# Two hybrid blocks on one core: the mixers' projections and gates as three products of rounded parts, in another order

## What is computed

```python
h = z @ w_in
(q_a, k_a, v_a, r_a, lr_f, lr_b, q_b, k_b, v_b, g_a, g_b) = jnp.split(h, SPLIT_POINTS, axis=-1)
a = gla_branch(q_a, k_a, v_a, r_a, lr_f, lr_b, gla_w2, gla_b2, gla_gn)
b = attention_branch(q_b, k_b, v_b, q_norm, k_norm, cos, sin)
y = (jax.nn.sigmoid(g_a + b_merge[0]) * (a @ w_pa)
     + jax.nn.sigmoid(g_b + b_merge[1]) * (b @ w_pb))
return y @ w_out
```

## Time and profile before

| | us |
|---|---|
| runs of the kernel | 2798.41, 2788.34, 2796.54 |
| median | 2796.54 |
| the profiled execution | 2796.98 |
| its span, first to last instruction | 2795.2 |
| TensorE busy | 2577.6 (92%) |
| VectorE busy | 1010.1 (36%) |
| ScalarE busy | 824.5 (29%) |
| GpSimd busy | 902.2 (32%) |
| mean granted TensorE clock | 0.965 |

### The profile page before, as it was taken

How to read it: one execution, slowest core, us unless ns; L and a number is a source line. 1 busy time by engine, 2 the same in 40 slices (tenths; PEclk the granted TensorE clock), 3 DMA queues, 4 the chain that set the end, 5 groups by cost and what they waited for, 6 DMA issues and landing times.

```text
span 2795.2 us, 46739 instructions
## 1 busy us (share of the span) xinstructions
PE 2577.6 (92%) x18898; PEld 2057.0 (74%) x18898; DVE 1010.1 (36%) x2406; ACT 824.5 (29%) x1416; POOL 902.2 (32%) x373
## 2 busy tenths in 40 slices
PE   7999999999999999999989799998978679999997
PEld 7997567999999766799989555555558575555554
DVE  3411433543442153354245532323234533232233
ACT  4431212444433131254433221221123522212112
POOL 6870002788788100178867000000016230000000
PEclk9999989999999999999999899999988989999999
DMA  7545321554654522145554899999963058999996
GB/s 236 170 157 148 118 58 61 162 170 158 189 181 146 152 98 61 61 151 183 173 143 125 330 417 421 421 421 422 421 206 103 19 215 353 421 421 421 422 421 258
DMA packets 287879, 644.01 MB, mean 230 GB/s; under 512 B 35584, under 2 KB 209792, under 8 KB 238336
## 3 DMA queue, kind: packets, MB, share of 16 engines
q1 hardware_dynamic: 284672, 635.79, 61.5%
q10 hardware_dynamic: 2176, 3.15, 0.4%
q0 software_dynamic: 896, 3.15, 0.4%
HBM read 637.85 MB, written 4.19 MB: 230 GB/s over the span
## 4 chain that ended last, share of the span: by engine, by line
PE 80%; DMA 10%; DVE 6%; ACT 2%; issue 1%; SPq 0%; ACTq 0%; POOL 0%; DVEq 0%
PE bank L558 37%; DMA wring<-in_exp_w 10%; PE bank L522 10%; PE bank L1088 6%; PE bank L1066 6%; PE bank L652 5%; PE bank L1099 3%; PE bank L1045 3%; PE bank L1058 3%; PE bank L740 1%; PE bank L591 1%; PE bank L813 1%; DVE ARENA L1919 1%; DVE XN_rounded L1527 1%; PE bank L532 1%
## 5 line engine op out<-in xcount | busy, mean ns | idle before, releaser
L1976 POOL TENSOR_TENSOR wring_rounded<-wring,wring_rounded 128x1024 fp32r<-128x1024 f32 (+1 forms) x336 | 873.7, 2613 | 320.2 <-ACT wring_rounded L1159 319.7
L558 PE MATMUL bank<-SQ_rounded,wring_rounded 128*128 128x272 f32 (+1 forms) x3456 | 647.9, 288 | 28.9 <-POOL wring_rounded L1976 18.0
L558 PEld LDWEIGHTS bank<-SQ_rounded,wring_rounded 128*128 128x128 f32 x3456 | 544.5, 190 | 31.2 <-POOL wring_rounded L1976 14.0
L558 PE MATMUL bank<-XN_rounded,wring_rounded 128*128 128x272 f32 (+1 forms) x1728 | 496.2, 287 | 0.0
L1159 ACT ACTIVATE wring_rounded<-wring 128x1024 fp32r<-128x1024 f32 (+1 forms) x336 | 374.7, 1116 | 351.7 <-PE bank L558 343.3
L558 PE MATMUL bank<-ARENA_rounded,wring_rounded 128*128 128x272 f32 (+1 forms) x3456 | 438.3, 289 | 9.5 <-DVE ARENA_rounded L1735 4.2
L558 PEld LDWEIGHTS bank<-ARENA_rounded,wring_rounded 128*128 128x128 f32 x3456 | 433.6, 190 | 12.7 <-DVE ARENA_rounded L1735 4.4
L558 PEld LDWEIGHTS bank<-XN_rounded,wring_rounded 128*128 128x128 f32 x1728 | 329.1, 190 | 0.1
L1088 PE MATMUL bank<-wring,ARENA 128*32 128x512 f32 x2048 | 246.2, 598 | 41.0 <-DVE ARENA L1919 30.2
L1427 ACT ACTIVATE ARENA<-bank 128x512 f32<-128x512 f32 x128 | 76.4, 597 | 672.3 <-PE bank L1088 672.3
L1066 PE MATMUL bank<-ARENA 64*128 64x256 f32 x2048 | 255.7, 389 | 1.6 <-ACT ARENA L1419 1.6
(11 more groups left out here) (242 smaller groups left out, 2455.9 us busy)
## 6 DMA issues: line engine op xcount, KB each, us to landing
wring<-in_exp_w SPq DMA_DIRECT2D x256, 1024.0 KB, 18.3
ARENA<-in_exp_w SPq DMA_DIRECT2D x128, 1024.0 KB, 16.8
wring<-in_ffn_w_gate SPq DMA_DIRECT2D x44, 1024.0 KB, 5.5
wring<-in_ffn_w_up SPq DMA_DIRECT2D x44, 1024.0 KB, 8.1
wring<-in_ffn_w_down SPq DMA_DIRECT2D x32, 1408.0 KB, 6.2
wring<-in_w_in SPq DMA_DIRECT2D x14, 2048.0 KB, 7.8
wring<-in_conv_w_in SPq DMA_DIRECT2D x24, 512.0 KB, 5.4
wring<-in_attn_w_in SPq DMA_DIRECT2D x5, 2048.0 KB, 8.0
```

Of the source, the lines that this page charges most:

```text
L558: ins = nc.tensor.matmul(o, rounded(a_[:, k, cols]), rounded(x), start=(start and k == 0 and j == 0), stop=(stop and k == len(tiles) - 1 a ...
L1976: st.done(nc.gpsimd.tensor_tensor(rounded(low), low, part(high), ALU.subtract), wl_ready)
```

## The change

The products of in4, in0, in1, in2 and of the gates become three products of rounded parts. Their chunks (16 for the projections, 16 for the gates in each layer) enter the plan of chunks; ScalarE makes the high parts, VectorE the low parts (a new `low_part`), with their own semaphore. The mixer's input is split too: ScalarE rounds XN into SQ, VectorE subtracts SQ from XN in place once the float32 products of in3 are done. v_a is now computed by channel in four tiles, copied out, and turned by TensorE into the layout by token. The key product of in3 goes first, the decays' products ahead of the queries; the means come after the first GLA tile, the swaps after v_a. Squares, QB, XR, OSTD and KET get other places in memory. On ScalarE absolute value, exponential and logarithm are put between the GLA tiles, and the three high parts of pb go to the steps 22, 24 and 26. VectorE's chain of norms, decays and rotations is reordered with low parts between them. GpSimd makes two pb low parts ahead of the last attention output's, and one after it.

```diff
+ROUNDED_BY_VECTOR = ("in4", "in0", "in1", "in2", "gate")
+QUERY_BANKS, KEY_BANK, GLA_BANKS = (2, 0, 4, 5), 1, (3, 6, 7, 3)
+VALUE_BANKS, TURN_BANKS, R_BANKS = (6, 7, 3, 6), (7, 3, 6), (7, 3, 6, 7)
+NORM_ORDER = ((4, KEY_BANK),) + tuple(enumerate(QUERY_BANKS))
...
+GATE_HIGHS = [1] + [n + 1 for n in range(STEPS) for g in GATES_DONE[n] if 2 <= g <= 12]
...
+                    low, high = chunk_views(c)
+                    pe.wait_ge(*low_at[c])
                     for k in range(KD):
-                        ins = nc.tensor.matmul(bank[b][:, 0:T], v[:, k, m * P:(m + 1) * P], XN[:, k, :], start=(k == 0),
-                                               stop=(k == KD - 1))
+                        for j, (a_, x) in enumerate(((low, SQ), (high, XN), (high, SQ))):
+                            ins = nc.tensor.matmul(bank[b][:, 0:T], rounded(a_[:, k, :]), rounded(x[:, k, :]),
+                                                   start=(k == 0 and j == 0), stop=(k == KD - 1 and j == 2))
...
+                tiles = pairs(SQ, XN, KD)
+                for m, b in enumerate(QUERY_BANKS):
+                    split_products(b, "act", tiles, "dve", (lambda k: st.need(xn_ready)) if m == 0 else None)
+                for m, b in enumerate(GLA_BANKS):
+                    split_products(b, "act", tiles)
+                    if m == 0:
+                        for i, mb in NORM_ORDER:
+                            products(mb, "act", None, [[(bank[mb][:, 0:T], const("mean64"), S2[:, i, :])]])
+                for b in VALUE_BANKS:
+                    split_products(b, "act", tiles)
+                for i, b in NORM_ORDER:
                     st.need(d2p)
-                products(i, "dve", "dve", [[(bank[i][:, 0:T], const("swap"), XR[:, i, :])]])
+                    products(b, "dve", "dve", [[(bank[b][:, 0:T], const("swap"), XR[:, i, :])]])
+                st.need(a2p)
+                for b, (a_, nt) in zip(TURN_BANKS, TILES):
+                    turns(b, "act", "act",
+                          [(bank[b][0:nt, m * P:(m + 1) * P], VT[:, m, a_:a_ + nt]) for m in range(4)])
+                for b in R_BANKS:
+                    split_products(b, "act", tiles)
...
+                for m, b in enumerate(R_BANKS):
                     st.need(bank_full["act"][b])
                     st.done(A(RA[:, m, :], bank[b][:, 0:T], ACT.Silu), bank_free["act"][b])
+                    high_part()
                 st.need(d2a)
                 A(QD[:, 0], BC[:, 0:2, :], ACT.Exp)
...
-                    if n in (22, 23, 24):
+                    if n in (22, 24, 26):
                         high_part()
...
+            def low_part():
+                c = next(vector_chunks)
+                low, high = chunk_views(c)
+                dve.wait_ge(wh_ready, c + 1)
+                st.done(TT(rounded(low), low, part(high), ALU.subtract), wv_ready)
...
+                low_part()
                 st.need(a2d)
                 for d in range(2):
                     st.done(STT(QD[:, d], QD[:, d], 0.125, QK[:, 0:2, :], ALU.mult, ALU.mult))
                     st.done(TT(KI[:, d], KI[:, d], QK[:, 2:4, :], ALU.mult))
                     st.done(TT(KE[:, d], KE[:, d], QK[:, 2:4, :], ALU.mult), gla_ready if d else None)
+                    low_part()
+                low_part()
+                low_part()
```

More of the change, by code:

```diff
@@ L268, in chunk_plan @@
         kind = label[0]
-        if kind == "up":
+        if kind in ROUNDED_BY_VECTOR:
+            for m in range(4):
+                add(label, lambda buf, m=m: buf[:, :].rearrange(
+                    "p (k n) -> p k n", k=KD)[:, :, m * P:(m + 1) * P], KD, P)
+        elif kind == "up":
             for ft in range(2):
@@ L431, in build_model @@
         chunks = chunk_plan(plan)
+        by_vector = [c[0][0] in ROUNDED_BY_VECTOR for c in chunks]
+        low_at = []
+        for c in range(len(chunks)):
+            n_vector = sum(by_vector[:c + 1])
+            low_at.append((wv_ready, n_vector) if by_vector[c] else (wl_ready, c + 1 - n_vector))
         def chunk_views(c):
@@ L673, in mixer @@
                 used(("in3", l))
-                v = cols_of(("in4", l), 512)
-                for m in range(4):
-                    products(4 + m, "act", "dve",
-                             [[(bank[4 + m][:, 0:T], v[:, k, m * P:(m + 1) * P], x) for k, x in enumerate(rows(XN))]])
-                used(("in4", l))
-                v = cols_of(("in0", l), 512)
-                for m in range(4):
-                    products(m, "act", "act",
-                             [[(bank[m][:, 0:T], v[:, k, m * P:(m + 1) * P], x) for k, x in enumerate(rows(XN))]])
-                used(("in0", l))
+                claim(0)
                 for i in range(4):
@@ new lines, in mixer @@
+                for m, b in enumerate(GLA_BANKS):
+                    copy(QK[:, m, :], b, bank[b][:, 0:T])
+                    high_part()
+                    if m == 0:
+                        for i, mb in NORM_ORDER:
+                            deviation(S2[:, i, :], mb, "eps_rms", T, a2d)
+                    elif m == 1:
+                        st.need(d2a)
+                        st.done(A(EL, GT, ACT.Abs))
+                        absolute = st.last
+                    elif m == 2:
+                        act.wait_ge(*absolute)
+                        st.done(A(EL, EL, ACT.Exp, scale=-1.0))
+                        exponential = st.last
+                    else:
+                        act.wait_ge(*exponential)
+                        st.done(A(EL, EL, ACT.Ln, bias=const("one")[:, 0:1]), a2d)
@@ L1322, in mixer @@
                             gate_tile(l, g)
+                    for _ in range(GATE_HIGHS.count(n)):
+                        high_part()
                     if n - 1 in OUT_STEPS:
@@ L1567, in mixer @@
                 st.done(v.tensor_copy(LR[32:48, :], bank[0][32:48, 0:T]), bank_free["dve"][0])
-                for i, b in ((4, 1), (0, 4), (1, 5), (2, 6), (3, 7)):
-                    st.need(a2d)
-                    st.done(v.tensor_copy(QB[:, i, :], bank[b][:, 0:T]), bank_free["dve"][b])
+                for _ in range(HIGHS):
+                    low_part()
+                dve.wait_ge(*last_use[("in3", l)])
+                for k in range(KD):
+                    st.need(xh_ready)
+                    st.done(TT(rounded(XN[:, k, :]), XN[:, k, :], part(SQ[:, k, :]), ALU.subtract), xn_ready)
                 for i in range(4):
@@ L1582, in mixer @@
                     st.done(STT(XR[:, i, :], QB[:, i, :], g, S2[:, i, :], ALU.mult, ALU.mult), d2p)
[L1583 to L1589 removed]
+                    if n in (1, 3, 4):
+                        low_part()
+                low_part()
                 st.need(a2d)
@@ L1674, in mixer @@
                         st.done(TT(AT[:, h, :], WB[:, 0:T], RA[:, h, :], ALU.mult), bank_free["dve"][WOVEN_BANK])
+                    for _ in range(GATE_HIGHS.count(n - 1)):
+                        low_part()
                 st.need(a2d)
```

131 lines of the change are left out of this document (66 added, 65 removed).

## The result

The changed kernel takes 2783.36 us (median of 9 runs, 2775.59 to 2784.55), the kernel before 2796.54; the ratio is 0.9948 (95% interval 0.9935 to 0.9961). That is 13 us faster. The forecast was 2762, 35 us faster, with a range of 2740 to 2784: the direction came out and the time lies just inside the range, but the gain was less than half of the forecast. The profiled execution took 2784.37 us.

The account below looks back on a forecast made before the run. TensorE, busy 92% of the span with products carrying the chain, was taken as the bound. Seam starts and woven stages of layers 0 and 1, -9.2 - 13.5 - 3.8 - 8.8 = -35.3 us on 2796.98, gave 2762; range 2740 to 2784.

Parts of the forecast that it names:

- Price of a product: Mixers' projections and gates: a tile falls from 3.66 to 3.03 us; the last projection ends 13.7 us earlier per layer.
- late low parts: Projections: VectorE's low parts 9, 10, 13, 14 and 15 come 0.1 to 0.6 us late, 1 us together.
- The seam: Between projections and woven stage: gate 0 waits 9.7 us for its low part; third gate starts 18.4 us after last r tile.
- The woven stage: Stage of attention, GLA and gates: 13.5 us shorter in layer 0 and 8.8 in layer 1, lasting 127 to 132 us.
- the chain: Woven stage's softmax steps: twelve low and high parts between them cost only +1 us per layer.
- -4.7 of layer 0: Woven stage, layer 0: rounded gates 0 and 1 take up the half-clock start of over 9 us before the stage, saving 4.7.
- The step that failed: Woven stage's clock: the remaining 24 us at the lower level stay, with -2 us for gates running there.
- Rival (a): Woven stage's clock falls further, lower-level time doubling from 24 to 48 us per layer: +12 per layer, 2786; chance 0.12.
- the prediction's own sign of being wrong: Among the signs that would refute the prediction: a woven stage's clock under 0.85.
- (b): Woven stage: low and high parts of twelve gates fully on the softmax chain, 27 us per layer, 2816; chance 0.06.
- (c): VectorE's low parts cost as on GpSimd, +1.13 us for some nine per layer, +20: 2782; chance 0.05.
- (d): Seam does not open because ScalarE's exponentials come earlier, -9.7 and -1.5 us, twice: 2740; chance 0.07.

Follow-up runs that it names:

- e1_seam: Changed kernel with VectorE making the low parts of gates 0 and 1 before the wait for the decays' exponentials; 2779.8 us.
- e2_proj_only: Changed kernel with the gates' part undone: one float32 product per k from the input's rounded high part, projections still rounded; 2769.4 us.
- e6_double: Changed kernel with extra scratch operations on VectorE and ScalarE behind each low and high part of the woven stage; 2780.1 us.
- e10_f32_loaded: The kernel of e2_proj_only with the engines' load of the woven stage's twelve low and high parts put back as scratch work; 2770.2 us.
- e4_refill_mid: Changed kernel with the first rounded product made five times more ahead of each of gates 7 to 13, no result changed; 2765.5 us.
- e3_refill_all: Changed kernel with the first rounded product made five times more ahead of each of gates 2 to 15, no result changed; 2791.8 us.
- e9_split: Changed kernel with a quarter of a gate moved into the middle of each stretch of the heads' outputs, no work added; 2807.8 us.
- e5: Changed kernel with gate 1's first product made 9 times more in layer 0 and 18 in layer 1, moving the woven stages; 2781.8 us.
- e14: Changed kernel with low parts of gates 0, 1 and 2 ahead of the exponentials' wait and layer 0's bias-table DMAs spread over the woven stage; 2766.3 us.
- e7_quarters: Changed kernel with the same 56 gate quarters dealt out otherwise: three in steps 10 to 19, two before, one behind; 2796.8 us.

## Why the prediction was right or wrong

- **Price of a product: right.** A projection tile took 3.03 us, the last r tile came 13.7 and 13.8 us earlier, as forecast. Twelve turns took 1.3 us (1.47 with the tail) for a forecast 1.5; the low part 1.22 us for 1.22; the late low parts 0.4 us for 1.
- **The seam: right.** Idle 9.5 us for 9.7, ended by VectorE's low part, in both layers; the third gate 18.8 us behind the last r tile for 18.4. That in layer 0 the bias table's DMAs pass under this wait was right too; e1_seam shows them as a wait of 7.5 us as soon as the idle is closed.
- **The woven stage: wrong, by its clock.** The terms outside the clock were right to 2 us: -8.8 for fourteen gates, +1.05 for the pb high part and +1 for the chain make -6.7 per layer, and length times clock fell by 9.0, with 2.2 us more idle on TensorE. The -4.7 of layer 0 came too, since the stage now starts at the full clock. The step that failed stood without a row: that the remaining 24 us at the lower clock stay 24 (the sum only took 2 us off for gates that run in them). They became 47.6 in both layers. Half of the difference is time, some 11.5 us per layer; the step was off by 11.3 and 11.2. Rounding the gates is what did it (e2_proj_only: the low time is back to that of the kernel before), the engines' load of high and low parts did not (e6_double, e10_f32_loaded), and extra full-array work in the middle undid it (e4_refill_mid).
- **Rival (a)** was this outcome with this size (24 to 48 us per layer, 2786) and had a chance of 0.12; the prediction's own sign of being wrong, a woven clock under 0.85, appeared with 0.83. The row that should have raised it was in the prediction: 0.71 in 390 to 425 with TensorE busy 32.9 of 35 us. A stage that loses clock with hardly any idle may lose it by what it computes, and the change took 17% off the gates' share of that. The rival's reason, less gate work between the small products, is only part of it: gates filled up to the old length got back 5 of some 24 us (e3_refill_all), and another order alone cost 24 (e9_split). The argument against the rival, that the stretches with smaller pieces kept 1.00, told of those stretches only, and they kept it in the changed kernel too.
- **Rivals (b), (c), (d)** did not occur: chain with slack, low part 1.22 us, seam open.

What stays open: which pattern of products lowers the clock. Float32 gates had under 35 us low in seven of eight profiled stages and 51.6 in one; rounded gates in the changed kernel's order had 47.6 in four and 26.9 to 57.6 in the eight of e1, e5, e6 and e14, and a gate filled up to the same length did not restore it. Whether a float32 product counts for more than rounded ones of the same length, or it is their place, was not separated.

## What to carry to other kernels

Read the granted clock of a stage before pricing an edit in it. Where it is below the full level with TensorE busy, time that is taken off the large products there may come back as clock, and length times clock tells what the edit itself did. When a cheap operation is put in front of the first product of a stage, follow the in-order queue of its engine: one wait ahead of it cost 9.5 us, and it moves to the next gate if only the first two are freed. Compare two kernels over all their runs, as span times clock and time at the lower level, before believing one profile. And try a burst of large products where the clock falls before reordering: here it paid 12 to 18 us three times, while two reorderings cost 13 and 24.

## What the runs showed of the hardware

- The clock fell to half with TensorE busy in every microsecond (4.00 of 4.00 us ahead of it), 1.3 us behind 3.08 us of products of 64 rows and 64 columns; behind a like stretch of the kernel before it stayed full for 15 us.
- It can stay low with TensorE busy all the time: for the last 20 us of e7_quarters' woven stages, at 0.50.
- 35 useless products of 272 columns per layer (4.4 us) made the kernel 17.9 us faster.
- The same products in another order had 83.3 in place of 47.6 us of a woven stage at the lower clock, and a shift by 1.1 or 2.3 us gave 31.7 or 50.8. Two profiled executions of the changed kernel, and both of its layers, agreed in the clock's two digits (0.83); two of the kernel before had 24.8 and 34.1 us in one stage.
- Eight DMAs of small rows issued on ScalarE held the activation behind them until 9.5 us after the start of the last exponential (317.6 against 308.1 in the changed kernel), and 7.5 us of that were a wait of TensorE once the seam was closed.
